# Expert weight loads that no longer wait for the first two row gathers

## Time and profile before

| | |
|---|---|
| time, 3 runs | 1161.29, 1163.33, 1164.15 us; median 1163.33 |
| span of the profiled execution | 1161.2 us (the page gives no time of its own beside it) |
| TensorE busy | 1067.6 us, 92% of the span |
| VectorE, ScalarE, GpSimd busy | 580.9, 404.3, 101.9 us |
| HBM read, written | 205.68 MB, 25.72 MB |
| weight loads of the experts | 32 each of gate, up and down, 1024 KB; median 21.8, 25.0, 26.6 us from issue to landing |
| granted TensorE clock, mean | 0.979 |

### The profile page before, as it was taken

The page is one execution under the profiler, slowest core; times in us unless marked ns, Lnnn a source line. Parts: engine busy times, 40 slices in busy tenths (PEclk is TensorE's granted clock), DMA queues, the critical chain, the costliest instruction groups (busy, mean ns, idle before and its releaser), DMA issues. The chain is left out here.

```text
span 1161.2 us, 13908 instructions
## 1 busy us (share of the span) xinstructions
PE 1067.6 (92%) x5491; PEld 773.1 (67%) x5491; DVE 580.9 (50%) x892; ACT 404.3 (35%) x795; POOL 101.9 (9%) x108
## 2 busy tenths in 40 slices
PE   3999999999999999999999999999995989877785
PEld 3688768888887787777886777788784433322232
DVE  3488725756444454451546666655557322212226
ACT  4442222222255655552227666423240111101104
POOL 1000012130000000000000100000031111111002
PEclk9999999999999999999999999999995999999998
DMA  8856744222522212214221212672657999999965
GB/s 302 273 187 227 247 150 127 73 64 70 173 84 82 82 64 91 82 62 129 73 82 64 70 55 60 270 304 72 253 186 300 404 421 419 420 420 421 419 267 236
DMA packets 71409, 226.16 MB, mean 195 GB/s; under 512 B 9389, under 2 KB 19942, under 8 KB 56882
## 3 DMA queue, kind: packets, MB, share of 16 engines
q1 hardware_dynamic: 64098, 209.40, 48.7%
q0 software_dynamic: 4464, 10.12, 2.3%
q10 hardware_dynamic: 2784, 5.77, 1.5%
HBM read 205.68 MB, written 25.72 MB: 199 GB/s over the span
## 5 line engine op out<-in xcount | busy, mean ns | idle before, releaser
L1119 PE MATMUL ps<-w_high,h_high 128*128 128x512 f32 x600 | 239.8, 400 | 0.5 <-ACT o_whole L1559 0.4
L1119 PE MATMUL ps<-w_high,h_low 128*128 128x512 f32 x600 | 234.2, 390 | 0.0
L1119 PE MATMUL ps<-w_low,h_high 128*128 128x512 f32 x600 | 233.6, 389 | 0.0
L1864 DVE TENSOR_TENSOR w_low<-w_loaded,w_high 128x2048 fp32r<-128x2048 f32 x44 | 101.3, 2303 | 110.9 <-ACT w_high L1512 110.9
L1119 PEld LDWEIGHTS ps<-w_high,h_high 128*128 128x128 f32 x600 | 112.9, 188 | 27.6 <-issue 4.2
L1119 PEld LDWEIGHTS ps<-w_high,h_low 128*128 128x128 f32 x600 | 112.6, 188 | 24.2
L1119 PEld LDWEIGHTS ps<-w_low,h_high 128*128 128x128 f32 x600 | 112.9, 188 | 22.2
L1358 PE MATMUL ps<-arena 128*64 128x512 f32 x448 | 103.4, 615 | 19.8 <-issue 19.8
L1512 ACT CAST w_high<-w_loaded 128x2048 fp32r<-128x2048 f32 x44 | 84.0, 1909 | 64.0 <-DMA w_loaded<-in_w_in 41.5
L1358 PEld LDWEIGHTS ps<-arena 128*64 128x64 f32 x448 | 35.1, 142 | 86.9 <-issue 86.9
L1620 ACT COPY arena<-ps 128x512 f32<-128x512 f32 x55 | 32.3, 588 | 153.8 <-PE ps L1119 153.3
(11 more groups left out here) (302 smaller groups left out, 1646.8 us busy)
## 6 DMA issues: line engine op xcount, KB each, us to landing
arena<-in_moe_w_gate SPq DMA_DIRECT2D x32, 1024.0 KB, 21.8
arena<-in_moe_w_up SPq DMA_DIRECT2D x32, 1024.0 KB, 25.0
arena<-in_moe_w_down SPq DMA_DIRECT2D x32, 1024.0 KB, 26.6
w_loaded<-in_w_in SPq DMA_DIRECT2D x27, 1024.0 KB, 6.1
arena<-in_w_ada SPq DMA_DIRECT2D x24, 1024.0 KB, 6.5
w_loaded<-in_w_in ACTq DMA_DIRECT2D x5, 1024.0 KB, 5.6
y_rows<-arena SPq DMA_DIRECT2D x10, 512.0 KB, 7.0
gates<-arena SPq DMA_DIRECT2D x20, 256.0 KB, 2.0
```

The lines of the kernel that those rows point to most:

```text
L1119: mm = pe.matmul(out, x[:, t, kk * P:(kk + 1) * P], w[w_buf(i)][:, k, :], start=(begins and k == 0 and j == 0), stop=(k == HK - 1 and j == ...
L1864: dve.tensor_tensor(w_lo[b][:], w_raw[b], w_hi[b][:].bitcast(F32), ALU.subtract).then_inc(w_split, 1)
```

```diff
@@ -915,8 +915,6 @@
             sp.wait_ge(pe_dense, last_of["wo1"] + 1)
             load_gate_or_up(1, 3, 3)
             load_gate_up(2, 2)
-            for x in ld_xg:
-                sp.wait_ge(x, 16)
             sp.wait_ge(x1_ready, 2 * NT)
             sp.wait_ge(st_h2_mid, 16 * 3)
             load_down(4, 4)
```

## The result

| | runs | median | lowest, highest |
|---|---|---|---|
| before | 20 | 1163.93 us | 1159.42, 1166.58 |
| after | 20 | 1165.26 us | 1161.83, 1169.37 |

The account below looks back on a forecast made before the run. Bound: the expert stage's stream of weights. The gather's 4.3 us of lateness less 2.3 of backlog made 2.0 us: 1161.2 to 1163.2 for the profiled execution, 1165.3 on the median of 1163.33; range 1161.5 to 1169.0.

Parts of the forecast that it names:

- The end hangs on the stream, the stream on the releases: Expert stage: the end follows from when pair 14's weights land; later loads wait until TensorE frees their slots.
- The width of the hole: Rival at the 6.65 us transfer hole: bytes moved by 891 alone set the end, saving 5 us and more; chance 0.06.
- The first gather lands late: GpSimd's first gather, issued at 883.46 among the early loads, lands 4.3 us later, at 892.0.
- TensorE late by the same amount: Pair 0's products end 4.3 us later, and every TensorE release in rounds 0 and 1 is 4.3 late.
- The slow rival: Gather pays 5.5 us and TensorE's clock rises later: TensorE 7.0 late, stream 4.7, end 1168.0; chance 0.24.
- The backlog hides 2.3 of it: At the gate load of 914.96, 2.3 us of queued transfers stood ahead, offsetting that much of the lateness.
- this release decide: Release of pair 4's gate load at 914.96, with the smallest backlog, sets the loss: 4.3 less 2.3, 2.0 us.
- pair 3's at 897.31: Release of pair 3's gate loads: 4.3 less 2.8 of backlog, 1.5 us, part of the 2.0 and not added.
- a ceiling: With TensorE unchanged, the weight stream could come forward by at most 2.3 us, rather less with row stores and gathers.
- signs of being wrong: Gather landing within 6 us, clock rising at another distance from the products' start, or pair 4's gate load finding a backlog.
- The hardly slowed gather: Rival: engines alternate evenly, the first gather is 0.8 us late, the stream gains 1.5, end 1161.8; chance 0.14.

Follow-up runs that it names:

- late_before: Kernel before, with twelve dependent GpSimd operations put ahead of the gathers to delay them: 1185.56 us, ratio 1.0197.
- warm_before: Kernel before, with 50 extra identity products, results unused, in four gaps of TensorE's routing work: 1164.69 us, ratio 1.0013.
- warm_longer: Changed kernel with extra identity products as in warm_after, but 21 instead of 16 in the last gap: 1163.73 us, ratio to before 1.0013.
- late_after: Changed kernel with the same delay of the first gather as late_before: 1183.34 us, ratio to before 1.0185.
- down_only: Kernel before, with only down block 4 moved ahead of the wait for both gathers: 1162.49 us, ratio 0.9996.
- first_gather: Changed kernel, but after down 4 SyncE waits for the first gather alone, then sends up 4 and g2: 1161.39 us, ratio to before 0.9992.
- warm_after: Changed kernel with 18, 7, 8 and 16 extra identity products, results unused, in TensorE's gaps: 1163.3 us, ratio to before 1.0001.

## Why the forecast was right, and which of its terms were not

*The end hangs on the stream, the stream on the releases.* Shown by a late gather, which moves the end by its whole lateness (`late_before`), by an early TensorE, which gives nothing in time as long as a backlog stands ahead (`warm_before`), and by the unused transfer time, which goes with pair 14. The other half, that an earlier release in the changed kernel moves the end forward, is in the traces and not in the times (`warm_longer`).

*The width of the hole is not the gain.* Shown by `late_after`, 1.4 to 2.2 us for a hole of 6.65, and by `down_only` and `first_gather`, which move 2.5 and 4.9 us of transfers forward for 0.5 and 0.9 us of time.

*The first gather lands late.* Shown, but over-sized. I took 4.3 us of lateness, and it was 7.7 - 4.2 = 3.5. I had gone by the third gather's 9.7 us, which met the same traffic at its beginning, and had allowed too little for the first meeting its end, with 2.4 MB of the 3.15 still ahead.

*TensorE late by the same amount.* The products started 3.5 late and took 9.57 us at a clock that rose within them as before: 0.85 in 900:905 puts the rise at 901.5, 4.9 us after their start instead of 5.3. The releases were 3.3 late. I had forecast 4.3. The slow rival's second half, a clock that rises later, did not happen; in the seven kernels without extra products pair 0's took 8.67 to 9.72 us, so the clock's rise varies by about a microsecond from one execution to the next and not with the gather.

*The backlog hides 2.3 of it.* This is the other mis-sized term, and it was also put at the wrong release. The stage from the first gather to pair 14 grew by 223.67 - 221.36 = 2.3 us, so the backlog absorbed 3.3 - 2.3 = 1.0. I had taken 7.1 - 4.8 from the landing time at 914.96. After the change the same load lands in

```profile
DMA to landing us min/median/max: 7.0/7.0/7.0
```

although its release is 3.3 us later (us from issue to landing of the gate load at 920.35), and the share in 920:925 is 0.97. The excess over 4.8 is therefore no measure of a queue ahead of it; the row transfers that run beside it at that time, which are there in both kernels, are the likely reason. The prediction had this release decide, with 2.0 us of new hole, and pair 3's at 897.31 make 4.3 - 2.8 = 1.5 of them. It is the other way round: the whole 2.3 to 2.4 us arises ahead of pair 3's loads, and nothing is added at pair 4's. With a backlog of 2.8 us there, 3.3 us of lateness would have opened 0.5. The 7.6 us that pair 3's loads took to land was misread in the same way, for the third gather, issued at 890.54 and landed 9.7 us later, ran beside them; after the change it had landed before they were issued, and they take 4.8 us. The bytes would have given the right size: down 4, up 4, g2 and the third gather are 3.15 + 0.34 MB, 8.3 us at 419 GB/s, and put behind the issue of down 4 at 6.61 they are through at 14.9, against a release at 13.85. That estimate of 1.1 us agrees with the 1.0 above, with `first_gather`, whose release is as before and whose pair 14 starts 1.1 us earlier, and with the 1.2 us of `late_after`.

The two errors, 1.0 and 1.3 us, have cancelled: 4.3 - 2.3 = 2.0 was forecast, 3.3 - 1.0 = 2.3 stands in the trace, and 2.2 in the times. That the number hit is luck. That the sign and the size class were right is less so: the lateness lay within the 2.8 to 5.8 of the forecast, and the 2.3 us were called a ceiling that other traffic makes smaller. Of the signs of being wrong that I had named none came: the gather took more than 6 us, the clock rose at 4.9 instead of 5.3 us, less than the spread between executions, and the gate load of pair 4 found no backlog. The split into 3.3 and 1.0 is from one pair of traces; at pair 8 they lie 3.2 us apart, and 2.3 at pair 14.

*Other rivals.* The hardly slowed gather is refuted by 7.7 beside 4.2. It had leaned on the rule of transfer engines that take turns between the queues (the Trainium skill, "DMA: Bandwidth & Descriptors", Queues, rings and completion order). Once its packets flow, the trace is near what that rival made of the turns: 3.3 us from the first packet to the landing instead of 2.3, where 0.8 us of loss was expected. What it lacked are the 2.5 us by which the first packet is later. So a small transfer on another queue is not cheap beside a large one, at 7.7 us against 4.2. What holds the first packet back, no run here shows. The wide hole is refuted as above, and so is the slow side, with 3.3 us of lateness where it needed 5.8.

*The profiled pair.* Its 2.4 us look like a proof and are not. 2.07 of them arose before the change, 2.3 in the stage, and from pair 14 to the end the changed kernel's execution took 54.4 us against 56.4. Over all eleven traces that last piece lies between 54.4 and 57.5 us with no order in it that I can see. Only the many timed runs show the 2.2.

What stays open: how much the clock is worth, and what cost the profiled execution of `warm_after` 2 us after pair 8. `warm_longer` has in its trace all that the theory asks for, its releases as in the kernel before and pair 14 one microsecond earlier, and is not faster by its times. Whether unprofiled executions find the clock at another level was not seen.

## What to carry to other kernels

A wait that leaves a visible hole in the transfers can be guarding something small and urgent behind it. Ask what the freed transfers will meet, and where the next release stands: a hole is worth only the backlog that stood ahead of that release, here about 1 us out of 6.65. If the early loads can be put behind the urgent transfer, as in `first_gather`, the loss goes away. To size a backlog, add up the bytes that are issued ahead of the release and set them against it; a landing time serves only beside that of a load in an empty queue with the same company. And add up the unused transfer time of both traces before believing in any one release.

## What the runs showed of the hardware that was not expected

A gather of 0.34 MB took 4.2 us from issue to landing on idle transfer engines, 6.3 us with about 1.3 MB of earlier transfers still to pass and 7.7 with about 2.4 MB, and of these 3.5 us more, 2.5 lay ahead of its first packet; a dependent `pow` of GpSimd on 128x8 elements took 1.8 us (21.40 for twelve), more than twice what I had planned the delay with. With the transfers saturated, the way from a slot's release to the products of pair 14 came out alike within 0.8 us in seven kernels.
